# Two-layer attention and recurrent block: score products over all 128 rows, with keys stored twice beside zero rows

## What is computed

```python
# layer 0 (dsa_mixer), per block of 128 queries
logits = jnp.einsum('bthd,bsd->bths', qii, k_idx)           # 8 indexer heads
score = jnp.einsum('bths,bth->bts', jax.nn.relu(logits), wi)
_, idx = lax.top_k(score, topk)
s = jnp.einsum('bthd,btkd->bthk', qi, k_sel) * HEAD_DIM ** -0.5
p = masked_softmax(s, valid[:, :, None, :])
out = jnp.einsum('bthk,btkd->bthd', p, v_sel)
# layer 1 (nsa_mixer): three such attentions o_c, o_s, o_w per head
o = gi[..., 0:1] * o_c + gi[..., 1:2] * o_s + gi[..., 2:3] * o_w
# both layers: 4 heads over 256 memory positions
s = jnp.einsum('bshd,bnhd->bhsn', q, k) * HEAD_DIM ** -0.5
o_mem = jnp.einsum('bhsn,bnhd->bshd', jax.nn.softmax(s), v)
x = x + jnp.concatenate([tok, o_mem], axis=-1) @ w_o[i]
```

## Time and profile before

| | us |
|---|---|
| median of 3 runs | 4112.8 (4111.73 to 4142.71) |
| profiled execution, its own time | 4130.22 |
| span of the profiled execution | 4128.4 |
| TensorE busy | 3786.9 (92% of the span) |
| ScalarE, VectorE, GpSimd busy | 1405.7, 1640.1, 1523.0 |

### The profile page before, as it was taken

One profiled execution on the slowest core, in us unless ns is written; L12 is line 12 of the kernel. 1 busy time (PEld: TensorE's weight loads), 2 busy tenths in 40 slices (PEclk: granted clock), 3 DMA queues, 4 the chain that ended last, 5 costly groups with the idle time before them and its releaser, 6 DMA issues.

```text
span 4128.4 us, 47953 instructions
## 1 busy us (share of the span) xinstructions
PE 3786.9 (92%) x17554; PEld 2937.3 (71%) x17554; DVE 1640.1 (40%) x2641; ACT 1405.7 (34%) x2646; POOL 1523.0 (37%) x1362
## 2 busy tenths in 40 slices
PE   6898999899999899979998986888888889998998
PEld 4656888785555688858877875777777777457887
DVE  4853331223443333043205666655555551113321
ACT  3254332223333333233324544333333333013332
POOL 4234445431221444544453221333333323015444
PEclk8789999895555999989999997999999999999999
DMA  3101333320000233323331110101111102222332
GB/s 114 52 11 46 97 97 96 84 77 1 1 1 1 67 96 95 98 66 97 93 101 52 47 47 26 36 26 31 31 32 31 28 24 77 72 86 82 97 93 76
DMA packets 471305, 245.79 MB, mean 60 GB/s; under 512 B 13819, under 2 KB 468710, under 8 KB 471014
## 3 DMA queue, kind: packets, MB, share of 16 engines
q1 hardware_dynamic: 468464, 239.10, 20.2%
q10 hardware_dynamic: 2678, 4.53, 0.4%
HBM read 241.51 MB, written 2.10 MB: 59 GB/s over the span
## 4 chain that ended last, share of the span: by engine, by line
PE 83%; DVE 9%; ACT 3%; issue 2%; POOL 1%; ACTq 0%; DMA 0%; DVEq 0%; POOLq 0%
PE ps L424 15%; PE ps L425 15%; PE ps L426 15%; PE ps L1185 5%; PE ps L1205 5%; PE ps L448 4%; PE ps L1194 3%; PE ps L1835 2%; PE ps L1820 2%; PE ps L1751 2%; PE ps L1839 2%; PE ps L1752 2%; PE ps L1753 2%; PE ps L1387 1%; DVE arena L2119 1%
## 5 line engine op out<-in xcount | busy, mean ns | idle before, releaser
L408 POOL TENSOR_TENSOR w_lo<-ring,w_hi 128x512 fp32r<-128x512 f32 (+1 forms) x860 | 1126.7, 1331 | 1796.2 <-ACT w_hi L399 1796.2
L399 ACT ACTIVATE w_hi<-ring 128x512 fp32r<-128x512 f32 (+1 forms) x860 | 488.6, 617 | 1477.9 <-PE ps L426 1269.5
L424 PE MATMUL ps<-h_hi,w_hi 128*128 128x512 f32 x2136 | 855.3, 400 | 57.0 <-POOL h_lo L581 35.9
L426 PE MATMUL ps<-h_hi,w_lo 128*128 128x512 f32 x2136 | 840.3, 393 | 0.0
L425 PE MATMUL ps<-h_lo,w_hi 128*128 128x512 f32 x1744 | 683.2, 392 | 0.0
L424 PEld LDWEIGHTS ps<-h_hi,w_hi 128*128 128x128 f32 x2136 | 408.4, 191 | 161.0 <-issue 62.2
L426 PEld LDWEIGHTS ps<-h_hi,w_lo 128*128 128x128 f32 x2136 | 406.9, 190 | 86.7
L425 PEld LDWEIGHTS ps<-h_lo,w_hi 128*128 128x128 f32 x1744 | 330.7, 190 | 71.2 <-issue 3.6
L678 DVE TENSOR_TENSOR silu_g<-ps,silu_g 128x512 f32<-128x512 f32 x88 | 60.9, 692 | 611.8 <-PE ps L426 611.8
L425 PE MATMUL ps<-a_lo,w_hi 128*128 128x512 f32 x768 | 299.7, 390 | 0.0
L1280 POOL TENSOR_SCALAR arena<-arena 128x256 f32<-128x256 f32 (+4 forms) x224 | 118.3, 528 | 430.9 <-DVE arena L1240 430.9
(11 more groups left out here) (340 smaller groups left out, 6101.2 us busy)
## 6 DMA issues: line engine op xcount, KB each, us to landing
ring<-in_ffn_w_in SPq DMA_DIRECT2D x176, 512.0 KB, 3.8
ring<-in_w_in SPq DMA_DIRECT2D x96, 512.0 KB, 4.0
ring<-in_ffn_w_down SPq DMA_DIRECT2D x32, 512.0 KB, 3.6
ring<-in_ffn_w_out SPq DMA_DIRECT2D x32, 512.0 KB, 3.7
ring<-in_w_o SPq DMA_DIRECT2D x16, 512.0 KB, 3.7
ring<-in_w_branch_gdn SPq DMA_DIRECT2D x16, 512.0 KB, 3.6
ring<-in_nsa_w_in SPq DMA_DIRECT2D x15, 512.0 KB, 3.7
ring<-in_dsa_w_in SPq DMA_DIRECT2D x13, 512.0 KB, 3.9
```

Of the source, the lines that this page charges most:

```text
L399: act.activation(w_hi[:, (halves(u) + j) % PIECES, 0:n, :], slot(u)[:, j * n:(j + 1) * n, :], ACT.Copy) \
L408: pool.tensor_tensor(w_lo[:, q % PIECES, 0:n, :], slot(u)[:, j * n:(j + 1) * n, :], w_hi[:, q % PIECES, 0:n, :].bitcast(f32), ALU.subtract ...
L424: pe.matmul(dst, wh, hi(k), start=first and k == 0, stop=False)
L426: ins = pe.matmul(dst, wl, hi(k), start=False, stop=last and k == 2 * n - 1)
```

## The change

Scores now read all 128 partitions: the query tile holds both heads of the pair, and the key tile holds one head's keys in one half and zeros in the other, so the other head adds nothing. For this every key tile exists twice, with the keys in the even or the odd half: `k_dsa`, `ki_even` and `ki_odd`, `k_pad`, `k_cmp`, `k_mem`. The value products keep 64 columns; the value tiles get 64-wide gaps of zeros, which nothing reads in this version. ACT copies each half by itself, so one copy becomes two. POOL writes the zeros: one set in each layer between the memory norm and the splits of weights (`pool_zeros`), and in layer 1 `k_pad` after the last projection unit and ahead of the key copies (`pool_key_zeros`). Some tiles move to scratch space (`squares`, `square_sum`, `silu_g`).

```diff
+    def pool_zeros(pool, p, norm):
+        for k in range(KT - 4, KT):
+            pool.wait_ge(*tile_ready(norm, k))
+        pool.wait_ge(sig("mem_ready").sem, p["mem"] + KT)
+        pool.memset(silu_g[:, :, :], 0.0)
+        pool.memset(v_mem.rearrange("p m j (x n) -> p (m j) x n", x=3)[:, :, 1, :], 0.0)
+        if p["layer"] == 0:
+            pool.memset(v_dsa.rearrange("p i (x n) -> p i x n", x=3)[:, :, 0::2, :], 0.0)
+            pool.memset(k_dsa[:, :, :], 0.0)
+            pool.memset(ki_even, 0.0)
+            pool.memset(ki_odd[:, :], 0.0).then_inc(sig("pads_zero").sem, 1)
+        else:
+            for b in range(2):
+                pool.memset(v_tok[:, b].rearrange("p i (x n) -> p i x n", x=5)[:, :, 0::2, :], 0.0)
+            pool.memset(v_cmp, 0.0)
+            pool.memset(square_sum[:, 0:128], 0.0).then_inc(sig("pads_zero").sem, 1)
+
+    def pool_key_zeros(pool):
+        pool.wait_ge(unit_done.sem, p1["units"][-1] + 1)
+        for b in range(2):
+            pool.memset(k_pad[:, b], 0.0).then_inc(sig("pads_zero").sem, 1)
...
-                pe.matmul(ps[:, 4 + n % 2, 0:(i + 1) * P], qi_rot[half, h // 2, i * P:(i + 1) * P],
-                          ki_dup[half, 0:(i + 1) * P], start=True, stop=True).then_inc(sig("idx_logits").sem, 1)
+                pe.matmul(ps[:, 4 + n % 2, 0:(i + 1) * P], qi_rot[:, h // 2, i * P:(i + 1) * P],
+                          (ki_even, ki_odd)[h % 2][:, 0:(i + 1) * P], start=True, stop=True) \
+                  .then_inc(sig("idx_logits").sem, 1)
...
-        act.activation(k_dsa, ps[:, 1, :], ACT.Copy).then_inc(sig("dsa_copied").sem, 1)
+        act.activation(k_dsa[EVEN, 0, :], ps[EVEN, 1, :], ACT.Copy)
+        act.activation(k_dsa[ODD, 1, :], ps[ODD, 1, :], ACT.Copy).then_inc(sig("dsa_copied").sem, 1)
...
                 act.wait_ge(sig("nsa_dup").sem, 2 * b + g + 1)
-                act.activation(k_dup[:, b, g, :], ps[:, 2 * b + g, :], ACT.Copy).then_inc(sig("nsa_copied").sem, 1)
+                act.wait_ge(sig("pads_zero").sem, 3 + b)
+                for e in even_odd:
+                    ins = act.activation(k_pad[e, b, g, even_odd.index(e), :], ps[e, 2 * b + g, :], ACT.Copy)
+                ins.then_inc(sig("nsa_copied").sem, 1)
...
-                        us.append(dict(q=q_rot[half, pair, tok], k=k_dsa[half, 0:nk], bias=bias, nk=nk,
-                                       v=[v_dsa[:, j, :] for j in range(t + 1)], gate=None, clamp=False,
+                        us.append(dict(q=q_rot[:, pair, tok], k=k_dsa[:, hh, 0:nk], bias=bias, nk=nk,
+                                       v=[v_dsa[:, j, HD:P] for j in range(t + 1)], gate=None, clamp=False,
...
-                            u |= dict(q=q_rot[half, pair, tok], k=k_dup[half, br - 1, g, 0:nk], bias=cb, nk=nk,
-                                      v=[v_tok[:, br - 1, j, gcol] for j in range(t + 1)])
+                            u |= dict(q=q_rot[:, pair, tok], k=k_pad[:, br - 1, g, hh, 0:nk], bias=cb, nk=nk,
+                                      v=[v_tok[:, br - 1, j, at:at + HD] for j in range(t + 1)])
...
                 pool_mem_norm(pool, plans[f"proj{i}"])
+                pool_zeros(pool, plans[f"proj{i}"], plans[f"attn{i}"])
                 pool_proj(pool, plans[f"proj{i}"])
+                if i == 1:
+                    pool_key_zeros(pool)
```

More of the change, by code:

```diff
@@ L291, in build_program @@
     ckv_n = area.take(T)
-    k_dsa = area.take(T)
-    ki_dup = area.take(T)
-    v_dsa = area.take(NT, HD)
+    ki_even = area.take(T)
+    v_dsa = area.take(NT, 3 * HD)
     w_idx = area.take(NT, IDX_HEADS)
@@ L309, in build_program @@
     memn_at = area.at
-    k_dup = area.take(2, 2, T)
+    k_pad = area.take(2, 2, 2, T)
     gelu_h = area.take(2, 2, 32)
[L312 to L315, removed]
+    k_cmp = square_sum[:, 0:128].rearrange("p (g e c) -> p g e c", g=2, e=2)
+    v_cmp = square_sum[:, 128:448]
+    posT = square_sum[:, 448:512].rearrange("p (j l) -> p j l", j=2)
+    k_dsa = squares
+    ki_odd = square_sum
+    k_mem = silu_g.rearrange("p a (e n) -> p a e n", e=2)
+    v_mem_units = [v_mem[:, :, j, :].rearrange("p m (x n) -> p m x n", x=3)[:, :, 0::2, :] for j in range(MEM_PAIRS)]
+    EVEN, ODD = slice(0, HD), slice(HD, P)
+    even_odd = (EVEN, ODD)
     w1 = Area(scores_at).take(2, CMP_LEN // 2, P)
@@ L1093, in act_nsa @@
         for g in range(2):
-            act.activation(k_cmp[:, g, 0:NC], ps[:, 7, g * 32:g * 32 + NC], ACT.Copy).then_inc(sig("nsa_copied").sem, 1)
-        act.activation(v_cmp[0:NC].rearrange("p g d -> p (g d)"), ps[0:NC, 7, 64:64 + 2 * HD], ACT.Copy) \
+            for e in even_odd:
+                ins = act.activation(k_cmp[e, g, even_odd.index(e), 0:NC], ps[e, 7, g * 32:g * 32 + NC], ACT.Copy)
+            ins.then_inc(sig("nsa_copied").sem, 1)
+        act.activation(v_cmp[0:NC].rearrange("p (x n) -> p x n", x=5)[:, 1::2, :],
+                       ps[0:NC, 7, 64:64 + 2 * HD].rearrange("p (g d) -> p g d", g=2), ACT.Copy) \
            .then_inc(sig("nsa_copied").sem, 1)
@@ L1152, in units_of_layer @@
                     tok = slice(t * P, (t + 1) * P)
-                    h = 2 * pair + hh
-                    us.append(dict(q=q_mem[half, pair, tok], k=k_mem[half, pair, :], bias=const("causal")[:, 0:N_MEM],
-                                   nk=N_MEM, v=[v_mem[:, j, h * HD:(h + 1) * HD] for j in range(MT)], gate=None,
+                    at = P * hh
+                    us.append(dict(q=q_mem[:, pair, tok], k=k_mem[:, pair, hh, :], bias=const("causal")[:, 0:N_MEM],
+                                   nk=N_MEM, v=[v_mem[:, j, pair, at:at + HD] for j in range(MT)], gate=None,
                                    clamp=False, out=(half, tok), first=True, last=True, pair=PAIRS + pair, need=0))
@@ L1179, in pe_attention @@
             pe.wait_ge(sig("nsa_copied").sem, 7)
+        pe.wait_ge(sig("pads_zero").sem, (1, 4)[layer])
         for n in range(N + LEAD + LAG_V):
```

36 lines of the change are left out of this document (24 added, 12 removed).

## The result

The changed kernel takes 3958.05 us (median of 4, 3947.80 to 3966.89), beside 4120.94 us for the kernel before (median of 4, 4111.73 to 4142.71): ratio 0.9597, 95% interval 0.9548 to 0.9645. The forecast was 3936, within 3912 to 4015. The two profiled executions are 173.3 us apart (4130.2 and 3956.9), where the sum said 177. Nearly equal totals hide terms that went differently.

What follows compares the result with a forecast made beforehand. PE was taken to bound both attentions, mostly at 1.2 GHz in layer 1. Terms -160.5 (layer 1), -16 (layer 0), -8 (indexer), +2.5, +4.1 and +1 (fills, copies) gave -177: 3936 us from 4112.8, range 3912 to 4015.

Steps and rivals of the forecast that it cites:

- Part 1: Layer 1's attention: with full-row scores the clock rises and stays; 246.7 us at 2.4 GHz, +8 for a low start.
- what differs is how much of its work uses 64 rows: PE's clock: equally busy at 0.50 and 1.00, so the share of 64-row work was taken to decide it.
- Part 2: Both attentions on PE: 128-row scores and 128-wide transposes merge, 0.15 us a turn; -16.2 in layer 1, -9.0 in layer 0.
- scores' own lead unchanged: Attention scores on PE: no shrinking of their own lead was counted, 0 taken, 11 us at most.
- turns whose transpose is 31 wide keep it: Attention turns with 31-wide transposes: they keep the drain, so only 108 turns in layer 1 and 60 in layer 0 merge.
- Part 3: Layer 0's attention: 104.8 us with merging, plus 3 for the low clock at its start, against 124: -16.
- Part 4: Indexer: two heads queue with 128 rows, but the clock rises some 4 us in; -8 us.
- low-clock alternative of +4: Indexer at 1.2 GHz: pairs of heads queue with 128 rows, costing +4 us in all.
- Part 5: POOL's zero fills and ACT's doubled copies: +2.5 at layer 0's fills, +4.1 for `k_pad`, +1 for other copies.
- Rival 1: Whole kernel: the clock stays as it is; only drains, indexer, zeros and copies count, -17, 4095 us; chance 0.10.
- rival 3: POOL's fills: far slower than its computing, so PE stands still; 4166 us at 30 ns per element; chance 0.02.
- rival 2: Layer 1's attention: the clock rises in about half only, falling back in light turns; +72, 4010 us; chance 0.08.

Runs made afterwards that it cites:

- e1: The changed kernel with layer 1's attention scores (branches, compressed and memory keys) reading the 64 rows of their own head again; 4112.08 us, ratio 0.9965.
- e2: The changed kernel with 0.75 instead of zero in every pad of layer 1's keys; 3957.87 us, ratio 0.9596.
- e6: e1 with value products of 128 columns in both layers; 3962.9 us, run once.
- e10: e6 with each of layer 1's half-row score products issued twice in a row to the same place; 4156.17 us, run once.
- e9: The changed kernel with an added product of 64 rows over 8 keys between each score and its transposes in layer 1; 4044.87 us, run once.
- e12: The changed kernel with half-row scores again in both branches of layer 1 (96 of 160 units); 4004.48 us, run once.
- e7: The changed kernel with the indexer's products on 64 rows again, both attentions left full; 3963.26 us, ratio 0.9590.
- e8: The changed kernel with layer 0's fills moved behind the first two units' splits and the branch-key fills one split earlier on POOL; 3947.82 us, ratio 0.9553.
- e3: The changed kernel with layer 1's scores made for only the first 64 queries of each tile (128 rows, 64 columns); 3924.14 us, ratio 0.9522.
- e4: The changed kernel with half-row scores again in layer 1's window branch alone (48 of 160 units); 3960.1 us, run once.
- e5: The changed kernel with value products of 128 columns in both layers; 3915.87 us, ratio 0.9473.
- e11: The changed kernel with the edits of e5 and e8 together; 3907.27 us, ratio 0.9483.

## Why the prediction was right or wrong

**Part 1, the clock in layer 1: right in size and in what decides it for this edit, too simple in why.** The prices at 2.4 GHz read from layer 0 and from one fast stretch of layer 1 held to within 0.01 us (values 0.36 and 1.01), and the low start, put at +8, was 22 us at half pace, about +11. Full rows raised the clock (e1 against the changed kernel), and rows of zeros do as well as rows of 0.75 (e2). But the step "what differs is how much of its work uses 64 rows" left something out: e6 has the same half-row scores as e1, and its clock rises and stays. More half-row work brings it down again (e10), and borders alone don't (e9). That borders work together with half rows is the reading that I prefer, but it is argued: e6 has wider value products too, and no run parts the two. Not settled either: why the kernel before holds 1.00 in layer 0 with half rows in all scores and falls in layer 1. Its five falls there (1017, 1075, 1133, 1191 and 1249 us) all come at the tenth turn of a pair's 24, behind the light turns over 31 and 128 keys, and those of e1, e9, e10 and e12 at the eighth to twelfth; layer 0 has no 31-key turns. The end of e10 holds where its start did not. No run here isolates that.

The forecast set a rule against this: by the Trainium skill (TensorE: Matmul & The Clock Gate, part 1) the clock follows how busy PE is. The measured stage stands against the records' busy time as the measure: 400.38 of 403.13 us busy at 0.56 in e1, 214.30 of 216.00 at 1.00 after. The records call PE equally busy in both, so busy time alone doesn't foretell the clock here.

**Part 2, the drain and the merging: right.** 0.15 per merging turn was 0.147 (91 + 56 ns). Two choices in it: "scores' own lead unchanged" was right; "turns whose transpose is 31 wide keep it" was wrong. They lose 0.114 (91 + 23), 48 x 0.114 = 5.5 us more; a 31-wide transpose behind a full score has no border either. With -5.5 and +3 for the start, 238.5 becomes 236, measured 237.9.

**Part 3, layer 0: -19 for -16.** The clock was high at the first score, so the +3 for a low start didn't come: 106.3 against the 107.8 of the sum. The other half is where the stage before ends: 125.3 to the next product, where the sum took 124.

**Part 4, the indexer: -7.8 for -8, by two misses that cancel.** The first and the second pair of heads, before and after (before, the two heads' products lie side by side in one row; after, each head has its own):

```profile
104.90 1.23 PE L968 MATMUL ps<-arena 64*128 64x256 f32 x4
106.59 1.49 PE L968 MATMUL ps<-arena 64*128 64x256 f32 x4 [0.47 <-ACT arena L992]
```

```profile
107.75 0.65 PE L1005 MATMUL ps<-arena 128*128 128x256 f32 x2
109.88 0.70 PE L1005 MATMUL ps<-arena 128*128 128x256 f32 x2 [1.05 <-ACT arena L1034]
```

The clock was at 1.00 from the first product on (it rose at 107.0), not 4 us in. Against that, the second pair starts 2.13 after the first, where it was 1.69: ACT's first relu stands behind its doubled copies of the indexer's keys, and PE waits 1.05 for it. At full pace PE's period is 1.81 for 1.71 of columns, so PE ends last and DVE waits 0.20, where the step had them level. The low-clock alternative of +4 didn't come. e7 confirms the term by itself: 8.0 at the accumulation, 7.7 at layer 0's first score.

**Part 5, fills and copies: fills 3.8 for 2.5, `k_pad` 4.1 for 4.1.** A fill costs 0.95 us for 1024 elements and 0.52 for 512, 0.84 ns an element and 0.1 fixed. The term that was off is the first: the 1 us of cover after the first split wasn't there. In the kernel before, PE's first product already started at 63.78, within the record of the L867 pair and 1.5 us behind the start of the split. In the changed kernel it waits for that split, 2.7 us after the last other thing it had to do:

```profile
PE ps L428 <- POOL w_lo L412: 2.7, 1, 2.7
```

so all of the fills' delay (3.7 us, 62.27 to 66.01) came through. `k_pad` cost what was said, +4.1: the zeros of 3.54 us start with the end of the split, the first half copy 1.9 later, the last ends 6.7 after it, where the last copy ended 2.6 after the split before. e8 shows that both were a matter of place: 3.9 and 3.2 of it go away by another order on POOL. Layer 1's first fills were hidden, as said. ACT's doubled copies show as the wait in the indexer's first pair (part 4); ahead of the indexer they cost nothing that can be told apart: its first product is 2.9 us later for fills of 3.8, since the products before it ran at the higher clock.

**What the sum didn't have: +9.3 in the rest of the kernel.** Compared instruction by instruction, ACT runs even with the kernel before until 880 us after the attention (0.2 us apart) and is 10.6 us later 18 us on; the instructions are the same. The stretch in both, before and after:

```profile
2228.50:2259.50 31.00, 27.00 (x175) 24.42 (x175) 17.37 (x36) 10.28 (x16) 5.94 (x4) 0.89 0.14 39
```

```profile
2046.00:2077.00 31.00, 26.99 (x121) 26.13 (x122) 12.51 (x24) 8.79 (x14) 3.11 (x2) 0.51 0.07 18
```

In the kernel before the clock was low for 6.8 us there, in the changed kernel for 30.7, in a stage with nothing changed (its products of weights and 128 columns take 415 ns instead of 275). The change by itself doesn't bring it, since all of these kernels contain it: e1, e3, e4, e6 and e12 have 6.8 us low at about this place, e2, e5, e7, e8, e9, e10 and e11 have 31 to 34, and the rest of the kernel takes 2777 to 2782 us in the first group and 2789 to 2793 in the second. Each of these is one profiled execution. No single edit divides the two groups; whether it is drawn anew at each execution was not tried, and its 10 us are half of the scatter of the changed kernel's own times (3948 to 3967).

**The total.** The forecast median of 3936 took 4112.8 less the sum; the kernel before measured 4120.9 beside the changed one, which is 8 of the 22 us between 3936 and 3958; its ratio of 0.957 lies within the measured interval. The other 14 are the gain: 162.9 between the medians for a sum of 177. Of these, 4 separate the sum from the two profiled executions (173.3), and 10 come of the profiled execution before, which lies 9 above its median. That sum and trace agree within 4 us is partly luck: the terms of the sum brought 182.5, and the 9.3 of the rest, which it didn't have, took most of the difference back. Rival 1 (clock unchanged) and rival 3 (slow fills) are out by the first trace; rival 2 didn't come in the changed kernel, but e12 shows what it would have looked like, at 96 half-row units.

## What to carry to other kernels

When TensorE is busy by the records and its clock is low, look at the shapes. Here products that left half of the rows unused went with the low clock, the more of them the lower; what stands around them counts too, but whether it is the borders between shapes was not settled. Padding a 64-row product with rows that add nothing costs no columns and gave 162 us here. Neighbouring groups on PE do better in the same array shape: each border between 64- and 128-wide groups cost about 0.15 us at 2.4 GHz, and removing most of those left (e5) was worth another 42 us for zeros that were already laid out. Zeros are cheap but stand in a queue: put them where the engine is idle, not where it is the one that others wait for.

## What the runs showed that was not expected

- The clock had high or low stretches at the same place with the same instructions: 6.8 or about 31 us low at 880 to 911 us after the attention, worth some 10 us. Differences of that size between single profiled executions of this kernel say nothing about an edit until the stage where they arise is found.
- With half rows and two borders a turn the clock took 65 us to rise (e6), with full rows and two borders 22 in the changed kernel and e2 and 9.5 in e7 and e8, with full rows and almost no borders 14 (e5) and 13 (e11). The start of a stage is worth several us either way.
- A product of 64 rows over 8 keys between full-array groups cost 0.47 us a turn (e9), more than the columns of a 256-key score (0.43).
- Products of 128 rows and 64 columns on different output halves run beside each other (e3): the stage shortened by 27 us with the same number of instructions and half of the scores' results.
